# RWKV scan in a two-block transformer kernel: the operations of a unit in another order on TensorE, VectorE and ACT

## What is computed

```python
def _rwkv7_step(S, inp):
    r, w, k, v, kk, a = inp
    sa = jnp.einsum('dbhij,dbhj->dbhi', S, -kk)
    S = S * w[..., None, :] + sa[..., None] * (kk * a)[..., None, :] + v[..., None] * k[..., None, :]
    y = jnp.einsum('dbhij,dbhj->dbhi', S, r)
    return S, y
# seq: (r, r), (decay, decay), ... forward and flipped; 512 steps
_, ys = lax.scan(_rwkv7_step, S0, seq)
y = ys[:, 0] + flip(ys[:, 1])
```

## Time and profile before

| | |
|---|---|
| median of three runs | 2921.2 us (2907.03, 2922.02, 2921.2) |
| the profiled execution | 2919.39 us |
| its span | 2917.6 us |
| TensorE busy in the span | 2758.9 us, 95% |
| VectorE busy | 1515.9 us, 52% |
| ACT busy | 865.9 us, 30% |
| mean granted TensorE clock | 0.979 of full speed |
| the scan, its first right product to its last state product | 556.30 to 788.25 us |

### The profile page before, as it was taken

How to read it: one execution, slowest core, us unless ns; L and a number is a source line. 1 busy time by engine, 2 the same in 40 slices (tenths; PEclk the granted TensorE clock), 3 DMA queues, 4 the chain that set the end, 5 groups by cost and what they waited for, 6 DMA issues and landing times. The chain is left out here.

```text
span 2917.6 us, 39032 instructions
## 1 busy us (share of the span) xinstructions
PE 2758.9 (95%) x16683; PEld 2192.4 (75%) x16683; DVE 1515.9 (52%) x2117; ACT 865.9 (30%) x1156; POOL 354.9 (12%) x334
## 2 busy tenths in 40 slices
PE   7999999888899899999999999899999899999998
PEld 6888877577665777788887785688887575688887
DVE  5555454677676833555544415463354655452343
ACT  3222233321144123322222425432222434422222
POOL 1111010211010001111100002120120100120110
PEclk9999999999999999999999998899999999999999
DMA  5555541000030023355444210223343210232231
GB/s 152 167 161 162 172 134 50 19 3 3 31 96 15 29 88 101 105 155 176 151 167 155 84 54 24 73 87 101 109 151 109 65 44 1 73 101 95 93 101 58
DMA packets 264317, 271.15 MB, mean 93 GB/s; under 512 B 9631, under 2 KB 245126, under 8 KB 263951
## 3 DMA queue, kind: packets, MB, share of 16 engines
q1 hardware_dynamic: 248784, 206.78, 22.9%
q0 software_dynamic: 15360, 61.87, 6.3%
HBM read 266.53 MB, written 2.10 MB: 92 GB/s over the span
## 5 line engine op out<-in xcount | busy, mean ns | idle before, releaser
L920 DVE TENSOR_TENSOR mix_wl<-ring_raw,mix_wh 128x2048 fp32r<-128x2048 f32 (+2 forms) x66 | 153.1, 2320 | 221.4 <-ACT mix_wh L807 221.3
L707 PE MATMUL mix_ps<-h_mix_hi,mix_wh 128*128 128x512 f32 x624 | 244.2, 391 | 0.0
L709 PE MATMUL mix_ps<-h_mix_lo,mix_wh 128*128 128x512 f32 x624 | 242.8, 389 | 0.0
L807 ACT ACTIVATE mix_wh<-ring_raw 128x2048 fp32r<-128x2048 f32 (+2 forms) x66 | 117.6, 1782 | 212.5 <-PE mix_ps L713 162.1
L707 PE MATMUL ffn_ps<-h_rw_hi,ffn_wh 128*128 128x512 f32 x448 | 175.3, 391 | 0.0
L709 PE MATMUL ffn_ps<-h_rw_lo,ffn_wh 128*128 128x512 f32 x448 | 174.3, 389 | 0.0
L920 DVE TENSOR_TENSOR mlp_wl<-ring_raw,mlp_wh 128x2048 fp32r<-128x2048 f32 (+1 forms) x38 | 96.7, 2545 | 131.1 <-ACT mlp_wh L807 131.1
L920 DVE TENSOR_TENSOR mlp_wl<-mlp_raw,mlp_wh 128x2048 fp32r<-128x2048 f32 x36 | 93.2, 2589 | 133.2 <-ACT mlp_wh L807 133.2
L713 PE MATMUL mix_ps<-h_mix_hi,mix_wl 128*128 128x512 f32 x624 | 154.2, 389 | 0.0
L707 PE MATMUL mlp_ps<-view,mlp_wh 128*128 128x512 f32 x384 | 149.7, 390 | 0.0
L709 PE MATMUL mlp_ps<-view,mlp_wh 128*128 128x512 f32 x384 | 149.4, 389 | 0.0
(11 more groups left out here) (605 smaller groups left out, 6018.8 us busy)
## 6 DMA issues: line engine op xcount, KB each, us to landing
ring_raw<-in_mlp_w SPq DMA_DIRECT2D x32, 1024.0 KB, 5.3
mlp_raw<-in_mlp_w SPq DMA_DIRECT2D x32, 1024.0 KB, 5.4
ffn_sraw<-in_ada_w POOLq DMA_DIRECT2D x34, 768.0 KB, 5.1
ffn_raw<-in_ffn_w_gu SPq DMA_DIRECT2D x44, 512.0 KB, 5.1
ring_raw<-in_ffn_w_gu SPq DMA_DIRECT2D x44, 512.0 KB, 4.7
mix_sraw<-in_ada_w POOLq DMA_DIRECT2D x22, 768.0 KB, 5.1
ring_raw<-in_w_in SPq DMA_DIRECT2D x14, 1024.0 KB, 5.2
ring_raw<-in_a_w_in SPq DMA_DIRECT2D x12, 1024.0 KB, 5.2
```

The lines of the kernel that those rows point to most:

```text
L707: nc.tensor.matmul(ps[:, it.banks[t], :], w(h, k, t), xh[:, k, :], start=it.first and k == it.k0, stop=False)
L709: nc.tensor.matmul(ps[:, it.banks[t], :], w(h, k, t), xl[:, k, :], start=False, stop=False)
L807: nc.scalar.activation(slot(wh, it), slot(raw, it), ACT.Copy).then_inc(hi_ready, 1)
L920: nc.vector.tensor_tensor(slot(wl, it), slot(raw, it), slot(wh, it).bitcast(F32), ALU.subtract)\
```

## The change

No instruction that computes is added or taken out. The table is gone; the order of a unit is written out call by call. Functions that did both halves or several parts in one call are split (`begin`, `turned`, `values`, `mask_out`, `update` into `update` and `turn`, `exps`, `turned_out`), and each of the five semaphores of the inversion becomes a pair, one for each half (the stage's reservation goes from 45 to 50). `update` no longer waits for earlier updates of its own engine. TensorE:

```diff
-                for b, (kind, kl) in enumerate(BEATS):
-                    if u > 0 and b < 8:
-                        chain(u - 1, b)
-                    if b == 4:
-                        products(u, 0)
...
+                before(0)
+                right(u, 0, 0)
+                right(u, 0, 1)
+                before(1)
+                products(u, 0)
+                left(u, 0, 0)
+                before(2)
+                left(u, 0, 1)
+                before(3)
+                turned(u, 0)
+                right(u, 1, 0)
+                right(u, 1, 1)
+                turned(u, 1)
+                before(4)
+                left(u, 1, 0)
+                left(u, 1, 1)
+                before(5)
+                right(u, 2, 0)
+                products(u, 1)
+                right(u, 2, 1)
+                left(u, 2, 0)
+                values(u, 0)
+                before(6)
+                left(u, 2, 1)
+                right(u, 3, 0)
+                before(7)
+                values(u, 1)
+                right(u, 3, 1)
+                left(u, 3, 0)
+                added(u)
+                left(u, 3, 1)
+                right(u, 4, 0)
+                if u + 1 < U:
+                    begin(u + 1, 0)
+                right(u, 4, 1)
+                left(u, 4, 0)
+                if u + 1 < U:
+                    begin(u + 1, 1)
+                left(u, 4, 1)
```

The waits of the inversion, for one of the functions:

```diff
             def left(u, kl, q):
 
-                i = (u * K + kl) * 2 + q
-                pe.wait_ge(w_out, i + 1)
+                pe.wait_ge(w_out[q], u * K + kl + 1)
                 if kl > 0:
-                    pe.wait_ge(x_out, (u * (K - 1) + kl - 1) * 2 + q + 1)
+                    pe.wait_ge(x_out[q], u * (K - 1) + kl)
...
-                last.then_inc(t_done, 1)
+                last.then_inc(t_done[q], 1)
```

More of the change, by code:

```diff
@@ L1881 @@
 QCH = QL // CH
-BEATS = [(kind, k) for k in range(LEVELS - 1) for kind in ("both", 0, 1)]
 def level_columns(t, k, odd):
@@ L2018, in chain, with begin @@
                     last.then_inc(y_done, 1)
-            def begin(u):
+            def begin(u, part):
+                if part == 1:
+                    if u > 0:
+                        pe.wait_ge(b_out, u)
+                    for c in range(RT):
+                        for ch in range(QCH):
+                            for hd in range(2):
+                                m = (c * QCH + ch) * CH
+                                last = nc.tensor.matmul(pm[0][hs[hd], m:m + CH], ar[u % 3][hs[hd], c, ch, 0:CH],
+                                                        kb[u % 2][hs[hd], c, ch, CH:P], start=True, stop=True)
+                    last.then_inc(a_done, 1)
+                    return
                 pe.wait_ge(scaled, u + 1)
@@ L2032, in begin @@
                                                     ar[u % 3][hs[hd], c, ch, 0:CH], start=True, stop=True)
[L2033 to L2041, removed]
                 last.then_inc(a_done, 1)
@@ L2057, in products, with turned, values @@
                             last.then_inc(g_done, 1)
[L2059 to L2076, removed]
+            def turned(u, j):
+                pe.wait_ge(masked, 4 * u + j + 1)
+                for i in range(4):
+                    last = nc.tensor.transpose(pm[j][:, i * P:(i + 1) * P], kb[u % 2][:, 2 * j + i // QCH, i % QCH, :],
+                                               e.ident[:, :])
+                last.then_inc(k_done, 1)
+            def values(u, j):
+                if u >= QUARTERS:
+                    return
+                pe.wait_ge(masked, 4 * u + 3 + j)
+                for i in range(4):
+                    at_v = units[u][1] * QL + (i % QCH) * CH
+                    last = nc.tensor.transpose(pm[j][0:CH, i * P:(i + 1) * P],
+                                               v[:, 2 * j + i // QCH, at_v:at_v + CH], e.ident[:, :])
+                last.then_inc(v_done, 1)
             def added(u):
@@ L2097, in right @@
                     pe.wait_ge(ta_out, u + 1)
[L2098 to L2101, removed]
+                if u > 0 or kl > 0:
+                    pe.wait_ge(t_out[q], u * K + kl)
                 for m in range(4):
@@ L2119, in left, with before @@
                                                 group(wm, q)[hs[hd], m, :], start=True, stop=True)
-                last.then_inc(t_done, 1)
+                last.then_inc(t_done[q], 1)
             pe.wait_ge(logs_done, 1)
             keep_clock(nc, e, pc[0], 6)
-            begin(0)
+            begin(0, 0)
+            begin(0, 1)
             keep_clock(nc, e, pc[0], 6)
             for u in range(U):
-                for b, (kind, kl) in enumerate(BEATS):
-                    if u > 0 and b < 8:
-                        chain(u - 1, b)
-                    if b == 4:
-                        products(u, 0)
[L2132 to L2146, removed]
+                def before(phase):
+                    if u > 0:
+                        chain(u - 1, phase)
+                before(0)
[37 more added lines that the diff above has]
+                left(u, 4, 1)
@@ L2151, in _, with exps @@
         def _(act):
[L2152 to L2163, removed]
+            def exps(u, part):
+                if part == 0:
+                    act.wait_ge(logs_done, u + 1)
+                    if u >= 2:
+                        act.wait_ge(g_done, 4 * (u - 1))
+                        act.wait_ge(k_done, 2 * (u - 1))
+                    nc.scalar.activation(kb[u % 2][:, :, :, CH:P], chunks(inc3), ACT.Exp, scale=-LOG_DECAY_MAX)\
+                        .then_inc(exps_done, 1)
+                elif part == 1:
+                    arx = ar[u % 3][:, :, :, 0:CH]
+                    nc.scalar.activation(arx, arx, ACT.Exp, scale=LOG_DECAY_MAX).then_inc(exps_done, 1)
+                else:
+                    act.wait_ge(exps_done, 3 * u + 1)
+                    nc.scalar.activation(inc[:, :], inc[:, :], ACT.Exp, scale=LOG_DECAY_MAX).then_inc(exps_done, 1)
             def begun_out(u):
@@ L2305, in middle, with turn @@
                 nc.vector.tensor_tensor(level_blocks(group(wm, q), kl + 1, up), level_blocks(bank_of(q, kl + 1), kl + 1, up),
-                                        mask.to_broadcast([P, 4] + list(mask.shape[2:])), ALU.mult).then_inc(w_out, 1)
+                                        mask.to_broadcast([P, 4] + list(mask.shape[2:])), ALU.mult).then_inc(w_out[q], 1)
             def update(u, kl, q):
-                i = (u * K + kl) * 2 + q
                 odd = 1 - units[u][0]
                 xtq = level_columns(group(xt[u % 2], q), kl + 1, odd)
[L2313 to L2321, removed]
+                dve.wait_ge(t_done[q], u * K + kl + 1)
+                nc.vector.tensor_tensor(xtq, xtq, level_columns(bank_of(q, kl), kl + 1, odd), ALU.add).then_inc(t_out[q], 1)
+            def turn(u, kl, q):
+                dve.wait_ge(t_out[q], u * K + kl + 1)
+                nc.vector.transpose(group(x[u % 2], q), group(xt[u % 2], q)).then_inc(x_out[q], 1)
             def chain(u, phase):
@@ new lines, in _ @@
+                if following:
+                    logs(u + 1, 0)
+                middle(u, 0, 0)
+                middle(u, 0, 1)
+                before(1)
+                if following:
+                    logs(u + 1, 1)
+                mask_out(u, 0, 0)
+                before(2)
+                update(u, 0, 0)
+                mask_out(u, 0, 1)
+                update(u, 0, 1)
+                turn(u, 0, 0)
+                turn(u, 0, 1)
+                middle(u, 1, 0)
+                middle(u, 1, 1)
@@ new lines, in _ @@
+                if following:
+                    scale(u + 1, 0)
+                before(3)
+                before(4)
+                update(u, 1, 0)
+                before(5)
+                turn(u, 1, 0)
+                update(u, 1, 1)
+                middle(u, 2, 0)
+                turn(u, 1, 1)
+                mask_out(u, 1, 0)
+                middle(u, 2, 1)
+                update(u, 2, 0)
+                mask_out(u, 1, 1)
+                before(6)
+                update(u, 2, 1)
@@ new lines, in _ @@
+                turn(u, 2, 0)
+                middle(u, 3, 0)
+                if following:
+                    scale(u + 1, 1)
+                turn(u, 2, 1)
+                middle(u, 3, 1)
+                update(u, 3, 0)
+                if following:
+                    scale(u + 1, 2)
+                    scale(u + 1, 3)
+                turn(u, 3, 0)
+                update(u, 3, 1)
+                middle(u, 4, 0)
+                turn(u, 3, 1)
+                if following:
+                    begin(u + 1, 0)
+                    begin(u + 1, 1)
@@ L2392, in _ @@
+                middle(u, 4, 1)
+                if following:
+                    begin(u + 1, 2)
+                before(7)
+                update(u, 4, 0)
+                update(u, 4, 1)
             for phase in range(8):
```

56 lines of the change are left out of this document (30 added, 26 removed).

## The result

The changed kernel takes 2874.1 us (median of four runs, 2869.3 to 2897.8), the kernel before beside it 2921.6 (2907.0 to 2934.6). The ratio is 0.986, 95% interval 0.982 to 0.990: 1.4% faster. Timed again with six runs against ten, it is 0.9864, 0.9842 to 0.9885. 2874 us was forecast.

A forecast was written before the change was run, and what follows sets the result against it. The scan was taken as bound by waits in the inversion's loop, with no engine full. Gains of 40.6, 6.5 and 3.6 us made 50.7, cut to 47: 2872.4 us, or 2874 against the median; range 2862 to 2888, 8 in 10 2860 to 2898.

The forecast's parts named there:

- What bounds the scan: Scan, 225 of 2919 us: no engine full; the inversion's loop waits, VectorE 40.8 us for left products; floor TensorE's 23.0.
- Prices and walk: One scan unit walked in the new order at old start-to-start distances: forward unit 23.4 us, backward 22.2, against 29.6.
- The step that failed: GpSimd's `kd` in the scan, 4.2 us, starts after S3 and is needed a unit later; costed at nothing.
- Sum: Scan gains 40.6 us in units 1 to 6, 6.5 in unit 0, 3.6 in unit 7: 50.7, reduced to 47 for longer crossings.
- Unit 0 and unit 7: Scan's ends: unit 0, without chain, 18.2 us against 24.7; unit 7, without successor, 19.6 against 23.2.
- Semaphores at nothing: Half-wise semaphores in the scan cost nothing: `BO`'s second wait is hidden by ACT's idle time, `update` has a wait less.
- The clock: Scan's clock dips, a unit 1.5 us longer, should go as TensorE waits shrink; clock 1.00 in the scan.
- Rival (a), half of the gain: Scan: four heads of queues each 0.8 us late, 22 of the 47 us lost: 2896 us; chance 0.10.
- Rival (b), no overlap on VectorE: VectorE bounds the scan at whole durations, 25.5 us a unit, 15 us less gain: 2889 us; chance 0.02.
- Rival (c), slower: Scan: blocked queues put loop and chain in series, 34.3 us a unit, 33 us more: 2954 us; chance 0.04.
- (d), no change: Scan: release of the two `pm` banks sets the period, so order hardly matters: 2920 us; chance 0.06.
- TensorE's entries: Entering another tile shape costs TensorE 0.15 us; the new order has 9 per forward unit, not 7: 0.3 us more.

The follow-up runs named there:

- run 1: Kernel before, order untouched, the inversion's five semaphores made pairs and update without waits for older updates: forward units 29.63 us, scan 223.5 us, 1.8 shorter.
- Run 5: Changed kernel with GpSimd's work on the next unit started at X10, mid-unit: `b1` 0.69 us, forward units 23.5, scan 176.3 us instead of 182.4.
- run 4: Kernel before with GpSimd's work on the next unit started when B1 is done: `b1` 1.24 us in units 0 to 5, scan 228.7 us, 3.4 longer.
- runs 2 to 5: run 2, run 4, Run 5, and the kernel before with GpSimd's next-unit work started only when U31 is done: `b1` 0.68 us, scan 232.5 us.
- run 2: Kernel before with B0 ahead of L40 and B1 ahead of L41, not both ahead of L31: forward unit 28.17 us, scan 211.9 us, 13.4 less.
- run 7: Changed kernel with an extra, unread 128x512 transposition on VectorE ahead of M41 in each unit: forward units 25.15 to 25.20 us, scan 4.7 us longer.
- run 8: Changed kernel with B0 and B1 together ahead of L31 again: forward unit 25.9 us, 1.3 more, scan 192.8 us, 10.3 more.
- run 10: Kernel of run 9 with T1 right behind T0 on TensorE: forward units 23.4 us, backward 22.6, scan 176.7 us instead of 174.0.
- run 9: Changed kernel with GpSimd's next-unit work at M11, U40 ahead of b2 and C7, state cleared behind C6: scan 174.0 us; timed 2868.4 us, ratio 0.9835.

## Why the prediction was right

- **What bounds the scan.** Right. TensorE's idle time in the scan went from 41.2 to 6.4 us, the waits for left products went from 40.8 to 3.0 us, and a unit from 29.6 to 24.6 us. The semaphores alone give nothing (run 1).
- **Prices and walk.** Right to 0.1 us at the nine points from `R10` to `B1` in the table. I put that down to the prices: each was a distance between starts in the old trace, with the 0.15 for entering another tile shape and the overlap on VectorE in it, and not a duration. On VectorE the walk was looser: it had U01 done at 5.9 us and waits of 0.25 for `C2`, 0.5 for `R10` and 0.3 for `R11`, where in unit 3 U01 ends at 6.5 and the waits are none, none and 0.16. Slack took that half microsecond; at a head it would have counted.
- **The step that failed** is "GpSimd's `kd` starts when S3 is done and is needed a unit later, its 4.2 us under 19". It looked only at when the result is needed, and not at what runs beside it. In the new order S3 starts 2.7 us ahead of `b1` instead of 5.4, so GpSimd's tensor_tensor falls on `b1`: 1.07 us in each of units 0 to 5. Run 5 takes the collision away and gets the walk's numbers; run 4 makes it in the old order. It was there to be read: the first `b1` of the kernel before, with GpSimd at work, took 1.76 us against 0.69 for the seven others:

```profile
553.37 1.27 POOL L1971 TENSOR_TENSOR rws_kd<-rws_kd,view 128x512 f32<-128x512 f32 x1
...
553.43 1.76 DVE L2280 TENSOR_TENSOR rws_xt<-rws_xt,rw_levels 128x512 f32<-128x512 f32 x1
```

The Trainium skill (SBUF — State Buffer, Who interferes with whom) says that a VectorE instruction with two SBUF inputs contends with a GpSimd instruction that reads SBUF, and calls the port pair that the two share an exclusive lock. The rows agree: in the rows of runs 2 to 5 and of the changed kernel, the one that came second ended its own length, less 0.13 to 0.15 us, after the end of the other.
- **Sum.** The walk gave 50.7 us, with 3.7 taken off for unknown crossings: 47. Measured in the profiles: 42.0 (42.9 in the scan); between the medians: 47.5 at first and 38.7 timed again. The collision costs 182.4 - 176.3 = 6.1, and the turn of direction, which the walk also lacked, about 0.5. With both put in, the bare walk would have given 44. The reserve covered half of what the walk missed in the scan (50.7 - 42.9 = 7.8), and for another reason than the one given. That the median came out at 2874 is partly luck: the median of the changed kernel lay 3.3 us under its profiled execution; timed again it was 2880.7.
- **Unit 0 and unit 7.** Forecast at 18.2 and 19.6 us, measured 19.3 (with the collision; 18.2 without) and 19.9.
- **Semaphores at nothing.** Right by run 1. **The clock:** right, 1.00 in every window of the scan, and in all nine profiles of the new order; of the five of the old one, four show stretches of a lower clock in the scan, and run 2 none. These stretches in units 4 and 6 of the kernel before (mean 0.94 in each) cost some 3 of the 42.9 us. Why they come is open: a wait of 1.45 us for S3 at `B0` stands ahead of each, but it stands in unit 2 too, at full clock.
- **Rival (a), half of the gain.** Not so, but its places were real: 0.6 us at `M41` costs 0.6 a unit (run 7), and `B0` waits for S3 as soon as it stands earlier (run 8).
- **Rival (b), no overlap on VectorE.** Not so: operations still start 0.20 us apart at 0.28 long.
- **Rival (c), slower, and (d), no change.** Neither. The wait for `C5` on VectorE was 0.65 us, as walked. TensorE's entries: two more of them at 0.15 fit the walk up to `B1`; taking one out by moving `T1` made it worse (run 10).

What stays open: the share of each other step of the new order. Whole engines could not be exchanged one at a time, as `T0` ahead of `R10` on TensorE needs the mask ahead of `M10` on VectorE, and with one order old and the other new each would wait for the other. That was not tried.

## What to carry to other kernels

Where engines hand work to each other in a written-out order and none is full, walk one period with start-to-start distances from the trace, and look for the heads of queues; the walk can be right to tenths. At a head an operation counts in full, and what stands in slack costs little or nothing (0.6 us a unit at the head, 0 to 0.3 in the slack here). For every operation that comes to stand beside another engine's, ask what the two share, even if its result isn't needed for long: a GpSimd tensor_tensor beside a VectorE operation with two SBUF inputs stops one of them.

## What the runs showed of the hardware that was not expected

- VectorE and GpSimd exclude each other for whole instructions when GpSimd runs a tensor_tensor and VectorE an operation with two inputs in SBUF: `b1` 1.76 and 1.24 for 0.69, `logs0` 1.99 for 1.22, the state product 1.43 for 0.42. In the other direction, GpSimd's tensor_tensor took 1.72 and 1.61 for 1.27, and its four tensor_scalar 2.03 for 1.73 beside S0, which kept its 0.68 (run 9). Operations with an input in PSUM, masks and updates, kept their times beside it (the 128x512 masks 0.65 to 0.69, the 128x128 updates up to 0.29), and so did transpositions.
- With the work of a unit dense enough, TensorE's busy time equals the unit to 0.01 us, 23.30 and 22.04 (run 9); the sum from distances in the old trace was 23.0 and 21.9.
